# Product-key experts: more first products in parts, and their low parts shared between GpSimd and VectorE

## What is computed

```python
s = einsum('thcd,ckd->thck', q, subkeys)      # 8 heads, 2 halves, 128 keys
sv, si = top_k(s, 16)                         # and the best 16 of 16*16 sums: experts, cv
gate = softmax(cv)
act = gelu(einsum('cd,ced->ce', x, u_tab[experts]))
y = einsum('ce,ced->cd', act * gate, v_tab[experts])
```

## Time and profile before

| | us |
|---|---|
| time, median of 3 runs | 4122.79 (4118.95 to 4124.25) |
| the profiled execution's own time | 4121.33 |
| its span in the profile | 4119.5 |
| PE busy | 3774.0 (92%) |
| DVE busy | 1962.0 (48%) |
| ACT busy | 1102.6 (27%) |
| POOL busy | 314.8 (8%) |

### The profile page before, as it was taken

How to read it: one execution, slowest core, us unless ns; L and a number is a source line. 1 busy time by engine, 2 the same in 40 slices (tenths; PEclk the granted TensorE clock), 3 DMA queues, 4 the chain that set the end, 5 groups by cost and what they waited for, 6 DMA issues and landing times.

```text
span 4119.5 us, 58595 instructions
## 1 busy us (share of the span) xinstructions
PE 3774.0 (92%) x25020; PEld 2669.1 (65%) x25020; DVE 1962.0 (48%) x3541; ACT 1102.6 (27%) x1698; POOL 314.8 (8%) x203
## 2 busy tenths in 40 slices
PE   7889999999988899999999699898689999999986
PEld 6669988988867699888988465656543333333232
DVE  4368567768653675677686324454531111111112
ACT  2313244444523132444445112223110000000000
POOL 0003200000000032000000000111100000000000
PEclk9789999999997999999999899999889999999998
DMA  4434444445444343344444312111259999999993
GB/s 193 164 123 155 143 144 164 165 164 175 165 152 164 123 164 134 144 164 164 174 172 147 119 67 92 62 62 67 87 238 427 427 427 428 427 427 428 428 419 131
DMA packets 80732, 846.44 MB, mean 205 GB/s; under 512 B 8848, under 2 KB 11024, under 8 KB 12208
## 3 DMA queue, kind: packets, MB, share of 16 engines
q1 hardware_dynamic: 80464, 842.60, 52.2%
HBM read 841.52 MB, written 1.05 MB: 205 GB/s over the span
## 4 chain that ended last, share of the span: by engine, by line
PE 74%; DMA 13%; DVE 9%; ACT 3%; issue 1%; POOL 0%; SPq 0%; DVEq 0%; ACTq 0%
PE bank L85 73%; DMA ring<-in_w_gu_dram 12%; DVE arena L121 3%; ACT arena L111 2%; PE bank L98 2%; DVE arena L189 1%; DMA arena<-in_w_dn_dram 1%; DVE arena L183 1%; DVE arena L135 1%; DVE arena L129 1%; DVE arena L127 1%; DVE arena L153 1%; ACT L111 0%; DMA mq<-in_mq_dram 0%; DVE arena L195 0%
## 5 line engine op out<-in xcount | busy, mean ns | idle before, releaser
L85 PE MATMUL bank<-arena 128*128 128x32 bf16 (+8 forms) x9996 | 989.7, 300 | 84.6 <-DVE arena L121 43.9
L85 PEld LDWEIGHTS bank<-arena 128*128 128x128 bf16 (+4 forms) x9996 | 559.1, 125 | 502.2 <-issue 335.4
L111 ACT ACTIVATE arena<-bank 128x256 f32<-128x256 f32 (+2 forms) x484 | 223.3, 461 | 1638.2 <-PE bank L85 1302.1
L121 DVE TENSOR_TENSOR arena<-arena 128x512 bf16<-128x512 bf16 (+5 forms) x892 | 557.4, 659 | 80.2 <-ACT arena L111 65.9
L85 PE MATMUL bank<-ring,arena 128*64 128x512 f32 (+1 forms) x1968 | 515.8, 605 | 32.4 <-DMA ring<-in_w_gu_dram 26.8
L85 PE MATMUL bank<-xT,ring 128*128 128x256 f32 x2016 | 463.4, 388 | 22.2 <-DMA mq<-in_mq_dram 18.7
L85 PE MATMUL bank<-xhi,uhi 128*128 128x256 f32 x1552 | 453.4, 292 | 14.5 <-DVE arena L127 8.7
L85 PE MATMUL bank<-xlo,uhi 128*128 128x256 f32 x1552 | 437.2, 282 | 0.0
L85 PEld LDWEIGHTS bank<-xT,ring 128*128 128x128 f32 x2016 | 387.5, 195 | 76.5 <-issue 20.7
L85 PE MATMUL bank<-xhi,ring_rounded 128*128 128x256 f32 x1552 | 435.1, 280 | 0.0
L85 PEld LDWEIGHTS bank<-ring,arena 128*64 128x64 f32 (+1 forms) x1968 | 170.1, 147 | 368.7 <-issue 282.7
(11 more groups left out here) (117 smaller groups left out, 2976.2 us busy)
## 6 DMA issues: line engine op xcount, KB each, us to landing
ring<-in_w_gu_dram SPq DMA_DIRECT2D x74, 2048.0 KB, 25.4
arena<-in_w_gu_dram SPq DMA_DIRECT2D x66, 2048.0 KB, 24.5
ring<-in_peer_u_dram SPq DMA_DIRECT2D x128, 1024.0 KB, 6.6
ring<-in_peer_v_dram SPq DMA_DIRECT2D x128, 1024.0 KB, 5.0
arena<-in_w_dn_dram SPq DMA_DIRECT2D x39, 2048.0 KB, 24.0
ring<-in_w_dn_dram SPq DMA_DIRECT2D x31, 2048.0 KB, 23.5
ring<-in_w_hg_dram SPq DMA_DIRECT2D x14, 2048.0 KB, 7.8
ring<-in_w_mod_dram SPq DMA_DIRECT2D x12, 2048.0 KB, 7.8
```

Source lines behind the costliest of these rows:

```text
L85: i = self.e.matmul(o, l, r, start=start, stop=stop)
L111: self.e.activation(o, i, f, scale=scale, **kw).then_inc(self.sem, 1)
L121: self.e.tensor_tensor(o, a, b, op).then_inc(self.sem, 1)
```

## The change

`WHOLE` = 38: from chunk 38 on every chunk is in parts, so the twelve odd chunks 39 to 61 turn from whole to parts in each of the two layers. `next_high` gives for each chunk the one two places later in `parted`, whose high part ScalarE makes right after this chunk's gelu; for the even chunks under 34 that is again chunk c + 4, for 34 it is 38, for 36 it is 39, and from 38 on it is c + 2. GpSimd keeps the low parts of the even chunks under 64; those of the odd ones, 63 with them, go to VectorE. VectorE makes one-hots 0 and 1 first, then in turn n the odd low parts that fall to it (39, 41, 43 and 45 in turn 0, then 47, 49, 51, 53, 55, 57, 59, 61, 63 in turns 1, 3, 5, 7, 8, 10, 12, 14, 15), the second-table splits in turn 12, gate n, and one-hots n + 2. TensorE's list keeps its order.

```diff
+WHOLE = 38
...
-        parted = [c for c in range(128) if c % 2 == 0 or c >= BEFORE]
+        parted = [c for c in range(128) if c % 2 == 0 or c >= WHOLE]
         turn = {c: i for i, c in enumerate(parted)}
+        next_high = {parted[i - 2]: c for i, c in enumerate(parted) if i >= 2}
+        odd = [c for c in parted if c % 2 and c < BEFORE + 2]
...
-            for n in range(16):
+            for n in range(2):
                 dve_keys_hot(l, n)
                 dve_gates_hot(l, n)
-                if n >= 1:
-                    dve_gate(l, n - 1)
+            for n in range(16):
+                for c in odd:
+                    if (BEFORE - 16 + 9 * n // 8 if n else 0) <= c < BEFORE - 16 + 9 * (n + 1) // 8:
+                        split_u(V, l, c)
                 if n == 12:
                     dve_split_v(l, 0)
                     dve_split_v(l, 1)
+                if n < 15:
+                    dve_gate(l, n)
+                if n < 14:
+                    dve_keys_hot(l, n + 2)
+                    dve_gates_hot(l, n + 2)
             dve_gate(l, 15)
...
         def act_split_u(l, c):
-            if c not in turn:
-                return
...
             for c in range(TURNED - 2):
                 act_stage1(l, c)
-                act_split_u(l, c + 4)
+                if c in next_high:
+                    act_split_u(l, next_high[c])
...
             for c in range(TURNED - 2, BEFORE):
                 act_stage1(l, c)
-                if c + 4 < BEFORE:
-                    act_split_u(l, c + 4)
-                elif c + 2 >= BEFORE:
-                    act_split_u(l, c + 2)
+                if c in next_high:
+                    act_split_u(l, next_high[c])
...
             for c in parted:
-                if c < BEFORE + 2:
+                if c % 2 == 0 and c < BEFORE + 2:
                     split_u(G, l, c)
```

## The result

The changed kernel takes 4129.77 us (median of 22 runs, 4126.3 to 4132.59) against 4124.23 us of the kernel before (22 runs, 4117.16 to 4127.53). The ratio is 1.0016, with a 95% interval of 1.0009 to 1.0023: 6.6 us, or 5.5 by the medians. Forecast were +5.8 us (ratio 1.0014) and the case "a near balance within 0.2%"; the measured interval, 3.7 to 9.5 us, reaches a little over 0.2%.

What follows compares the result with a forecast made beforehand. TensorE's own work is three quarters of the span, but VectorE becomes the bound around the builds. Two layers of +2.9 us make +5.8 on the median 4122.79: 4128.6 us (+0.14%), range 4119 to 4137.

Steps and rivals of the forecast that it cites:

- a near balance within 0.2%: Whole kernel: gains and new waits nearly cancel, leaving the time within 0.2% of before; the forecast case, chance 0.6.
- The chain of high and low parts: Chunks 38 to 44: two buffers, prepared two chunks ahead, make TensorE wait 1.5 us three times; chunk 44 starts 2.65 later.
- VectorE's queue: Gate 0 to chunk 61's low part: VectorE's work plus standing beside POOL totals 72.0 us without idling, and sets TensorE's pace.
- The lock for VectorE's own low part: Odd chunks' low parts on VectorE are also stopped while POOL's operation runs; if not, 0.7 us a layer is saved.
- Build 13 and the clock: Second-table splits no longer stop build 13, giving back 2.7 us and the slow clock's 1.5 a layer.
- a fall of its own: Behind the 3.2 us wait ahead of build 14, TensorE's clock falls to 1.2 GHz, adding 1.5 us a layer.
- the sum's 9.9: After chunk 61's low part: TensorE's wake, chunk 61, build 15, chunks 62 and 63 take 9.9 us to the first second product.
- What follows stage 1 hangs on the end of chunk 63 and shifts with it: After chunk 63, everything moves by the stage's own delay, put at +2.8 to +2.9 us a layer.
- this very wait: TensorE idle 2.85 us in 536 to 542 with the clock at 1.00, cited to show not every wait brings a fall.
- A, VectorE keeps up: Rival for the builds' stretch: POOL's stops cost under about 0.7 us each, TensorE bounds, -6.5 us a layer, 4110; chance 0.1.
- 9.6 against 8.25 us for two builds: Between builds: VectorE's step of two builds with a low part takes 9.6 us, TensorE's new one 8.25, so VectorE bounds.
- a gain of 0.62 us a chunk: Odd chunks 39 to 61: each turned from whole (3.45) to parts (2.83) saves 0.62 us, 7.4 a layer if nothing is late.

Runs made afterwards that it cites:

- the fastest version: Changed kernel plus third high-part buffer, VectorE making all low parts from chunk 38, splits in turn 15, chunk 64's low part before chunk 2's splits: 4084.91 us.

## Why the prediction was right, point by point

**The chain of high and low parts.** Forecast: 1.5 us ahead of chunks 40, 42, 44, and chunk 44 2.65 us later. Measured: 1.49 three times, and 2.96. The measured period of two chunks is 7.22, against the 7.16 of the sum (two times 2.83 and 1.5). The prediction's own terms, 4.17 + 0.15 + 0.07 - 2.83, make 1.56 and not 1.5, and with 1.56 the period is the measured one. The first period is 7.35, because chunk 38 starts within the tail of the whole chunk 37. Taking the three chunks out (parts from 44 on) gives the loss back, as chunk 44 and layer 0's first second product show.

**VectorE's queue.** Forecast 72.0 us from gate 0 to chunk 61's low part, without idle time; measured 71.6, without idle time. It began 2.75 us later than before, counted from chunk 24 (forecast 2.7). The waits forecast ahead of builds 3, 5, 12 and chunk 53 (1 to 1.5) were 1.05, 1.37, 1.11 and 1.08, and that of 3.2 ahead of build 14 was 3.16. The two runs that move low parts from one engine to the other show the mechanism: with more work on VectorE a layer's last second product came 10.2 us earlier than in the changed kernel, with less of it 12.7 us later, against what the amount of VectorE's own work would say. Of the 10.2, 3.6 are there by chunk 44 and come from the shorter chain of high and low parts; with three buffers, where that chain makes no wait, moving the low parts to VectorE gives 10.6.

**The lock for VectorE's own low part.** The prediction took from a neighbouring row that it excludes GpSimd too. In the changed kernel none of them is caught beside a running GpSimd operation, and all last 1.22 to 1.23, so the 0.7 us never came up. But the row that the prediction took is borne out by the run with all low parts on GpSimd, where one of the two second-table splits, the same operation on the other table, is caught:

```profile
521.52 4.57 DVE L122 TENSOR_TENSOR ring_rounded<-ring,vhi 128x1024 fp32r<-128x1024 f32 x2
522.26 2.74 POOL L122 TENSOR_TENSOR ring_rounded<-ring,uhi 128x1024 fp32r<-128x1024 f32 x1 [2.06 <-ACT uhi L112]
```

The two splits take 4.57 us instead of 2.36, and end 1.09 after GpSimd does, 0.13 less than one such operation lasts. The reverse is in the changed kernel: VectorE's low part runs from 486.28, GpSimd's row starts at 487.06 and takes 2.70 instead of 2.36, 0.34 more; VectorE's ends at 487.50, so GpSimd's ends 0.10 earlier than if it had started then.

```profile
487.06 2.70 POOL L122 TENSOR_TENSOR ring_rounded<-ring,uhi 128x1024 fp32r<-128x1024 f32 x1 [4.86 <-ACT uhi L112]
```

**Build 13 and the clock.** The 2.75 us and the slow clock behind them are gone, and the wait ahead of build 14 brought a fall of its own, forecast at 1.5: from the end of chunk 61's low part to the first second product are 11.2 us instead of the sum's 9.9, which is 1.3. At that product the forecast was +2.8, and +2.34 was measured.

**What the prediction missed.** "What follows stage 1 hangs on the end of chunk 63 and shifts with it" is wrong in size. The 3.15 us behind chunk 63 are the same as before, but now the clock falls behind them: chunk 66 is 3.67 late where the first second product was 2.34 late, 1.3 us a layer. The prediction had used this very wait as its argument that not every wait brings a fall. So +3.75 a layer was measured where +2.9 stood, 7.5 us in the two stages against 5.8. That the time, +5.5 to +6.6, lies nearer to 5.8 is luck: what lies outside the stages varies by some us from one execution to the next, and the interval of 3.7 to 9.5 us holds both values.

**The chances.** The range of 4119 to 4137 held the time, and the balance within 0.2% was the likeliest case. The rival on the other side (A, VectorE keeps up, -6.5 us a layer) had the right value for a kernel in which VectorE does keep up: with VectorE doing all low parts, and two buffers still, it was -6.45.

What stays open is why the same wait behind chunk 63 brings a fall in some kernels and not in others. It does so in the changed kernel, with all parts on VectorE and two buffers, with all on GpSimd, with parts from 44 on, with a third buffer alone and (there behind 4.38 us) with the splits in turn 15; it doesn't in the kernel before, with the order alone, and with the third buffer and all on VectorE. Whether it comes was the same in both layers of each kernel and, for the two profiled again, in both executions; whether it lasts 3.4 or 6.8 us differed between layers in two kernels (parts from 44 on, splits in turn 15).

## What to carry to other kernels

Before work is moved to an engine with idle time on average, add up its queue over the stretch where it would run, with what another engine's operations make it stand, and compare the sum with the bound engine's: here 9.6 against 8.25 us for two builds decided it. When GpSimd and VectorE both run operations with two inputs in SBUF in the same stretch, GpSimd's help can cost more than it does: the fastest version takes it away, though that gives VectorE more work. And a gain of 0.62 us a chunk needs all its waits gone; half the repairs (buffers alone, splits alone) only brought the changed kernel back to about the time before, all together gave 0.9%.

## What the runs showed of the hardware

A GpSimd operation of 2.36 us with two inputs in SBUF stops VectorE's two-input operations in SBUF for its whole length less some 0.13 us (bf16 one-hots: a set of 4.90 for 2.68; float32 splits: 4.57 for 2.36), and a VectorE operation already running holds GpSimd back to about its end (2.70 for 2.36). VectorE operations with one input in PSUM are not affected (0.68 either way). Which waits of TensorE are followed by the 1.2 GHz level repeated from one execution to the next in the two kernels that were profiled twice, and depends on more than the length of the wait: 3.15 us behind chunk 63 are followed by it with all parts on VectorE and not once the third buffer is added. One such fall of 3.4 us costs 1.3 us behind chunk 63 (18.46 us instead of 17.12 from the first second product to chunk 66) and 1.7 where TensorE works right through it (chunk 59 in the kernel before, 5.2 us instead of 3.5).
